# Two heads' 64-row matmuls issued as a pair, from the upper and lower half of TensorE's rows

## The chip, the core and the metric

The kernel runs on one core of a Trainium2 chip. The metric is the device time of one execution in microseconds (us); lower is better. A core has five engines that run their own instruction streams and meet at semaphores: TensorE (PE, with its weight loads shown apart as PEld), VectorE (DVE), ScalarE (ACT), GpSimd (POOL) and SyncE (SP, which issues DMAs).

## What is computed

Two transformer-like blocks of two layers each, for 512 tokens of width 1024, all in fp32. Two places matter here. Both contract over a head dimension of 64, so their matmuls use 64 of the 128 rows of the array.

```
# block 0 (attention of the first block) and block 1 (dsa_attention), 8 heads of 64 each
s = einsum('bqhd,bkhd->bqhk', q, k) * 64 ** -0.5      # masked, softmax, times v
# block 1 only: the index score which picks the keys of block 1's attention
logits = einsum('bqhd,bsd->bqhs', iq, ik) * 64 ** -0.5
score  = einsum('bqh,bqhs->bqs', iw, relu(logits))    # summed over 8 index heads, then top-k of keys
```

## The kernel before

Each engine's program is written out by hand and its order is fixed. A *unit* is one 1024x128 slice of a weight matrix: TensorE multiplies it with the activations in eight k-steps of three matmuls each (high and low parts of an fp32 value kept as two fp32r tensors, `hH` and `hL`), 128x512 each, line L1758. Units alternate between two PSUM banks (`ACC`), and a unit can start only when `acc_free` says that VectorE or ScalarE has read the bank two units back.

**Block 0 attention.** 32 *steps* per layer: step n is head `n % 2` of the head pair `n // 2 % 4` of the query tile `i = n // 8`. The keys of tile i are the first 128(i+1), so a score matmul is 128 queries by 128, 256, 384 or 512 keys. Three steps go into each unit from the 13th on, behind its k-steps 0, 3 and 6. In one call `attention(w, n)` TensorE issues the scores of step n (L1961, into `SC[n % 2]`, banks 3 and 4), the transposes of the probabilities of step n-1 (L1972), and the product with v of step n-2 (L1983). VectorE reads the scores (L1352), ScalarE takes the exponential (L939) and copies the transposed tile (L948). The head pair's two heads lie in partitions 0 to 63 and 64 to 127 of `qT` and `kT`.

**Block 1 attention.** The same 32 steps, after the last projection unit, with matmuls of the output projection put between (`half_step`, L1932 to L1934) and in the first 16 steps one dummy matmul (`keep_warm`, L1898) per step. VectorE also finishes the top-k search here (`top_round`, L1632 and L1635).

**Block 1 index logits.** 32 logits matmuls per layer, y = 8 i + head, each 128 queries by 128(i+1) keys (`index_logits`, L1864). They are put between the k-steps of units 6 to 10 and 12 by the table `IX_AT`: for a unit with m of them, behind the k-steps 7-m to 6. Logits y go to bank `PT` (5) or `OA` (6) by the parity of y, so TensorE waits at y for ScalarE's relu of y-2 (L1166). VectorE adds each into the score (L1616, L1618); it holds the relus back through four buffers `ir`. In VectorE's program the scores of unit u+1 stand ahead of its reading of unit u (`pool_window`, first instruction L1320), which in turn frees the bank that unit u+2 waits for. ScalarE's relus of a unit stand behind the copy (L885) of the result of the `pool_window` before. Unit 11 is replaced by `pool_mix`, which writes banks 2 and 7 (`MIX`).

Of the kernel before, what the change touches and what calls it, by code (L numbers as in the profile page):

```python
# [27 lines left out]
ACT = mybir.ActivationFunctionType  # L28
AX_X = mybir.AxisListType.X

P = 128
# [11 lines left out]
HD = 64  # L43
# [103 lines left out]


IX_AT, _y = {}, 0
for _u, _n in ((6, 3), (7, 6), (8, 6), (9, 6), (10, 6), (12, 5)):  # L150
    IX_AT[_u] = tuple(range(_y, _y + _n))
    _y += _n
assert _y == 32


TOP_AT, TOP_STEPS, _r, _r3 = {}, {}, 0, 0
for _u in range(10, IN2):
    _n, _n3 = 1 + (_u >= 18), int(_u >= 12)
# [115 lines left out]
def build(nc, d):  # L274
    ctx = ExitStack()
    with ctx:
# [65 lines left out]
        with ExitStack() as share:  # L342
# [4 lines left out]
            iqT = sb("iqT", [P, 4, S], F32, share)  # L347
            ikT = sb("ikT", [P, S], F32, share)
            bias2 = sb("bias2", [P, 10 * P], F32, share)
            ir = sb("ir", [P, 4, S], F32, share)  # L350
# [19 lines left out]
        STAT = bank[2]  # L370
        DB = bank[0:3]
        SC = bank[3:5]
        PT, OA, TRO = bank[5:8]
        OSUM, R1, WARM = bank[5], bank[6], bank[4]
        THIRD, FOURTH = bank[5], bank[7]
        MIX = (bank[2], bank[7])

        def cst(name, a=0, b=None):
            o, n = CAT[name]
# [42 lines left out]
        turn_done = signal("turn_done", 12, 17, 2)  # L422
        sc_done = signal("sc_done", 32, 32)
        sc_read = signal("sc_read", 32, 32, 2)
# [32 lines left out]
        ix_done = signal("ix_done", 0, 32)  # L457
        ix_relu = signal("ix_relu", 0, 32)
# [53 lines left out]
        def att_step(n):  # L512

            return n // 2 % 4, n // 8, n % 2
# [327 lines left out]
        def _(act):  # L842
# [170 lines left out]
            for L in range(LAYERS):  # L1013
                w = Where(0, L)
                norm(w, 0)
                fourth_high(w, 0)
                for u in range(24):
# [27 lines left out]
                    if u in (19, 23):  # L1045
                        i = (u - 19) // 4
# [99 lines left out]
                for k in range(KD):  # L1146
                    for u in range(2):
                        y = 3 * k + u
                        next_high(w, 40 + y // 2, y % 2)
                    y = 3 * k + 2  # L1150
# [6 lines left out]
            for L in range(LAYERS):  # L1157
                w = Where(1, L)
                norm(w, 0)
                fourth_high(w, 0)  # L1160
                for u in range(IN2):
                    for y in IX_AT.get(u, ()):
                        wd = P * (y // 8 + 1)
                        act.wait_ge(ix_done.sem, ix_done.at(w, y + 1))
                        act.wait_ge(ix_used.sem, ix_used.at(w, y - 3))
                        act.activation(ir[:, y % 4, 0:wd], (PT, OA)[y % 2][:, 0:wd], ACT.Relu,  # L1166
                                       scale=HD ** -0.5).then_inc(ix_relu.sem, 1)
                    j = turn_of(1, u)
                    if j is not None:
                        turn_input(w, j, u // 2, u % 2, acc_of(w, u)[0], HD ** -0.5 if 5 <= j < 9 else 1.0)  # L1170
                    if u >= 2:
                        high_of(w, u + 2)
                    if 0 < u - POOL_U <= 4:
                        g = u - POOL_U - 1
                        piece_high(w, N_PD2 + g, piece[:, g % 2, :], pdH[:, g, :])
                    if u in (WPOOL + 1, WPOOL + 2):
                        for g in (0, 1) if u == WPOOL + 1 else (2, 3):
                            piece_high(w, N_PY2 + g, piece[:, g % 2, :], pdH[:, g, :])
                for n in range(SLOTS):
                    for h in HALVES_AT[n - 1] if n else ():  # L1180
                        first_half(w, h)
                    attention(w, n)
                use_table(ROOT)
                second_halves(w)
                output_root(w, 0)
                next_high(w, 14, 1)
                norm(w, 1)

                def hidden(c, i, s):

                    bk, n = (33 + s) % 2, N_HID2 + HCH * c + s
                    act.wait_ge(acc_free[bk].sem, acc_free[bk].at(w, i + 12 * c + 18 + s + 1))
                    act.wait_ge(piece_lo.sem, piece_lo.at(w, i * 2 + n - 1))
                    act.activation(piece[:, s, :], relu[:, s, :], ACT.Square).then_inc(piece_ready.sem, 1)  # L1194
                    act.activation(hidH2[:, bass.ds(i * 2 + s, 1), :], relu[:, s, :],
                                   ACT.Square).then_inc(piece_hi.sem, 1)

                fourth_high(w, 1)
                hidden(0, 0, 0)
                hidden(0, 0, 1)  # L1200
                for c in range(FCHUNKS):
                    with act.Fori(1 - c, HCH // 2) as i:
                        for s in range(2):
                            hidden(c, i, s)
                            next_high(w, i + 15 + 16 * c, s)
                    for k in range(KD):
                        bk = (49 + k) % 2
                        next_high(w, k + 23 + 16 * c, 0)
                        unit_wait(w, k + 23 + 16 * c, 1)
                        if c == 0:  # L1210
                            act.activation(mT2[:, k, :], ACC[bk][:, :], ACT.Copy).then_inc(acc_free[bk].sem, 1)
                        else:

                            act.wait_ge(acc_free[bk].sem, acc_free[bk].at(w, k // 2 + 12 * c + 26 + k % 2 + 1))
                            square(w, SQ_OUT[1][1] + k, k % 2, mT2[:, k, :])
                        if c == 0 or k < KD - 1:
                            next_high(w, k + 23 + 16 * c, 1)
                output_root(w, 1)
                next_high(w, 46, 1)
# [3 lines left out]
        def _(dve):  # L1223
# [297 lines left out]
            for L in range(LAYERS):  # L1521
                w = Where(0, L)
# [159 lines left out]
            for L in range(LAYERS):  # L1682
                w = Where(1, L)
                dve.wait_ge(rope_ready, 1)
                norm_scales(w)
                for u in range(IN2):
                    if u == 0:
                        copy_gates(w)
                    if u == 2:
                        gate_scale(w)  # L1690
                    for y in IX_AT.get(u + 1, ()):
                        index_score(w, y)
                    j = turn_of(1, u)
                    if j is not None:
                        turn_finish(w, j)
                    elif u != WPOOL:
                        pool_window(w, u - POOL_U)
                    if u in (WPOOL, WPOOL + 1):
                        for g in (0, 1) if u == WPOOL else (2, 3):
                            pool_scaled(w, g)  # L1700
                    for rounds in TOP_AT.get(u, ()):
                        top_round(rounds)
# [35 lines left out]
        def _(pe):  # L1738
# [115 lines left out]
                pe.wait_ge(sq_ready.sem, sq_ready.at(w, 8 + c + 1))  # L1854
                pe.matmul(STAT[:, :], cst("ones"), sq[:, c % 2, :], start=True, stop=True).then_inc(sq_used.sem, 1)

            def index_logits(w, y):
                i, h = y // 8, y % 8
                if y == 0:
                    pe.wait_ge(turn_done.sem, turn_done.at(w, 5))  # L1860
                if y >= 2:
                    pe.wait_ge(ix_relu.sem, ix_relu.at(w, y - 1))
                p0 = h % 2 * HD
                pe.matmul((PT, OA)[y % 2][:, 0:P * (i + 1)], iqT[p0:p0 + HD, h // 2, i * P:i * P + P],  # L1864
                          ikT[p0:p0 + HD, 0:P * (i + 1)], start=True, stop=True).then_inc(ix_done.sem, 1)

            def turn(w, j):
                src = turn_src(w.b, j)
# [31 lines left out]
            def pool_mix(w, g):  # L1900

                if g == 0:
                    pe.wait_ge(w_lo.sem, w_lo.at(w, WPOOL + 1))
                pe.wait_ge(piece_lo.sem, piece_lo.at(w, N_PD2 + g + 1))
                if g >= 2:
                    pe.wait_ge(piece_ready.sem, piece_ready.at(w, N_PY2 + g - 1))
                c = g * P
                pe.matmul(MIX[g % 2][:, :], pwH[:, c:c + P], pdH[:, g, :], start=True, stop=False)
                pe.matmul(MIX[g % 2][:, :], pwL[:, c:c + P], pdH[:, g, :], start=False, stop=False)
                pe.matmul(MIX[g % 2][:, :], pwH[:, c:c + P], pdL[:, g, :], start=False,  # L1910
                          stop=True).then_inc(unit_done.sem if g == 1 else pool_done.sem, 1)
# [40 lines left out]
            def attention(w, n, fill=()):  # L1952
                q, k, v, sc, pt, ao, st, _, n0 = ATT[w.b]

                for n_ in (n,) if n < 32 else ():
                    f, i, h = att_step(n_)
                    if n_ == 0:
                        pe.wait_ge(turn_done.sem, turn_done.at(w, (12, 17)[w.b]))
                    if 1:
                        pe.wait_ge(sc_read.sem, sc_read.at(w, n - 1))  # L1960
                    pe.matmul(SC[n_ % 2][:, 0:P * (i + 1)], q[h * HD:h * HD + HD, f, i * P:i * P + P],  # L1961
                              k[h * HD:h * HD + HD, f, 0:P * (i + 1)], start=True, stop=True).then_inc(sc_done.sem, 1)
                for i in fill[0:1]:
                    half_step(w, i // 4, i % 4, 0)
                m = n - 1
                if 0 <= m < 32:
                    f, i, h = att_step(m)
# [9 lines left out]
                if 0 <= m < 32:  # L1977
                    f, i, h = att_step(m)
# [115 lines left out]
            with pe.Fori(0, LAYERS) as L:  # L2094
                w = Where(0, L)
# [57 lines left out]
                with pe.Fori(0, KD // 2) as i:  # L2153
                    for m in range(2):
                        for u in range(3):
                            y = 3 * m + u
# [126 lines left out]
```

## Time and profile before

| | us |
|---|---|
| median of 3 runs | 3181.61 (3181.59 to 3187.2) |
| the profiled execution | 3177.61 |
| its span in the trace | 3175.6 |
| PE busy | 3011.6 (95% of the span) |
| DVE, ACT, POOL busy | 1252.0, 1147.7, 1246.4 |
| mean granted TensorE clock | 0.96 of full |

The profiled execution is 4.0 us below the median of the runs. Busy time of an engine is the time in which it has an instruction in work; waits stand apart. A granted clock of 1.00 is 2.4 GHz, 0.50 is 1.2 GHz.

### The profile page before, as it was taken

How to read it: one execution, taken by the hardware profiler on the slowest of the kernel's cores; microseconds unless marked ns; L12 is line 12 of the kernel's file. 1: busy time of each engine (PE TensorE's matmuls, PEld its weight loads, DVE VectorE, ACT ScalarE, POOL GpSimd, SP SyncE). 2: the span in 40 equal slices, each digit the busy share in tenths (PEclk: the TensorE clock that was granted, in tenths of full speed). 3: DMA queues.
4: the chain of work that ended last, by engine and by line, in shares of the span. 5: the costliest groups of instructions: out<-in, count | busy, mean ns of one | idle time of the engine just before them, and what ended most of it. 6: DMA issues, size and time to landing. Idle time of an engine off the chain costs nothing.

```text
span 3175.6 us, 42194 instructions
## 1 busy us (share of the span) xinstructions
PE 3011.6 (95%) x14156; PEld 2368.0 (75%) x14156; DVE 1252.0 (39%) x2240; ACT 1147.7 (36%) x1894; POOL 1246.4 (39%) x626
## 2 busy tenths in 40 slices
PE   9998899999999989999999998999999999999997
PEld 7767877788877678778888656678878656688876
DVE  4455426553064444265521467330012557330012
ACT  4453134443234522344433223542233223542331
POOL 3313123555432131235554343145553343145553
PEclk9999899999999988999999989999999989999999
DMA  3211012223311100112333111122222111022222
GB/s 128 67 41 34 1 40 67 93 94 100 104 64 66 40 27 1 47 67 93 99 99 100 56 47 54 34 73 93 92 93 86 58 44 60 31 72 97 92 93 93
DMA packets 62869, 217.35 MB, mean 68 GB/s; under 512 B 6577, under 2 KB 6705, under 8 KB 62481
## 3 DMA queue, kind: packets, MB, share of 16 engines
q1 hardware_dynamic: 62416, 214.48, 20.4%
q8 instruction: 82, 1.34, 0.2%
q0 software_dynamic: 320, 1.12, 0.1%
q14 instruction: 51, 0.41, 0.0%
HBM read 213.48 MB, written 2.10 MB: 68 GB/s over the span
## 4 chain that ended last, share of the span: by engine, by line
PE 80%; DVE 7%; POOL 4%; ACT 4%; issue 3%; DVEq 1%; ACTq 0%; DMA 0%; POOLq 0%; SPq 0%
PE bank L1758 48%; PE bank L2059 5%; POOL wL L681 3%; PE bank L1961 3%; PE bank L1932 2%; PE bank L1807 2%; PE bank L1785 2%; PE bank L1983 2%; PE bank L1933 2%; PE bank L1934 2%; PE bank L1864 1%; PE bank L1972 1%; ACT wH L850 1%; PE bank L1815 1%; PE bank L1872 1%
## 5 line engine op out<-in xcount | busy, mean ns | idle before, releaser
L681 POOL TENSOR_TENSOR wL<-raw,wH 128x1024 fp32r<-128x1024 f32 x380 | 920.2, 2422 | 1409.0 <-ACT wH L850 1409.0
L1758 PE MATMUL bank<-hH,wH 128*128 128x512 f32 x1744 | 728.9, 418 | 23.4 <-POOL wL L681 17.6
L1758 PE MATMUL bank<-hL,wH 128*128 128x512 f32 x1744 | 687.2, 394 | 0.0
L1758 PE MATMUL bank<-hH,wL 128*128 128x512 f32 x1744 | 686.9, 394 | 0.0
L850 ACT ACTIVATE wH<-raw 128x1024 fp32r<-128x1024 f32 x380 | 399.4, 1051 | 278.6 <-PE bank L1758 238.3
L1758 PEld LDWEIGHTS bank<-hH,wH 128*128 128x128 f32 x1744 | 331.5, 190 | 164.1 <-issue 87.4
L1758 PEld LDWEIGHTS bank<-hL,wH 128*128 128x128 f32 x1744 | 331.5, 190 | 72.2
L1758 PEld LDWEIGHTS bank<-hH,wL 128*128 128x128 f32 x1744 | 332.4, 191 | 69.2 <-issue 10.5
L1758 PE MATMUL bank<-hidH,wH 128*128 128x512 f32 x864 | 338.1, 391 | 2.4 <-POOL wL L681 2.3
L1758 PE MATMUL bank<-hidH,wL 128*128 128x512 f32 x864 | 336.3, 389 | 0.0
L1758 PE MATMUL bank<-hidL,wH 128*128 128x512 f32 x864 | 336.3, 389 | 0.0
L1717 DVE SCALAR_TENSOR_TENSOR relu<-bank,rstd 128x512 f32<-128x512 f32 x64 | 44.1, 692 | 479.8 <-PE bank L1758 467.8
L1758 PEld LDWEIGHTS bank<-hidH,wH 128*128 128x128 f32 x864 | 162.1, 188 | 41.9 <-issue 7.5
L1758 PEld LDWEIGHTS bank<-hidL,wH 128*128 128x128 f32 x864 | 162.2, 188 | 34.0
L1758 PEld LDWEIGHTS bank<-hidH,wL 128*128 128x128 f32 x864 | 162.2, 188 | 33.0
L1588 DVE SCALAR_TENSOR_TENSOR mT<-bank,par,mT 128x511 f32<-128x511 f32 (+1 forms) x176 | 131.9, 749 | 111.0 <-ACT mT L1127 96.5
L714 POOL TENSOR_TENSOR hidL<-piece,hidH 128x512 f32 (+1 forms) x108 | 139.5, 1293 | 75.7 <-ACT hidH L885 75.2
L939 ACT ACTIVATE sc<-sc,st 128x128 f32<-128x128 f32 (+3 forms) x128 | 71.9, 562 | 185.2 <-DVEq L1355 184.7
L1194 ACT ACTIVATE piece<-relu 128x512 f32<-128x512 f32 x64 | 40.4, 632 | 216.3 <-DVE relu L1717 215.6
L1961 PE MATMUL bank<-kT,qT 64*128 64x128 f32 (+3 forms) x256 | 104.1, 487 | 14.1 <-DVE v L1339 14.1
L726 POOL TENSOR_TENSOR eb<-ab,const 128x512 f32<-128x512 f32 x40 | 50.1, 1268 | 147.3 <-PE bank L2059 84.3
L1127 ACT ACTIVATE mT<-bank,par 128x512 f32<-128x512 f32 x88 | 68.5, 779 | 98.5 <-DVE bank L1584 94.2
(323 smaller groups left out, 4287.1 us busy)
## 6 DMA issues: line engine op xcount, KB each, us to landing
raw<-w_dram SPq DMA_DIRECT2D x398, 512.0 KB, 3.4
x<-x_dram SPq DMA_DIRECT2D x4, 512.0 KB, 9.0
out_dram<-x SPq DMA_DIRECT2D x1, 2048.0 KB, 6.2
const<-const_dram SPq DMA_DIRECT2D x1, 1421.0 KB, 12.8
par_next<-par_dram POOLq DMA_DIRECT2D x5, 168.0 KB, 2.6
qkT<-pos_dram POOLq DMA_DIRECT2D x1, 256.0 KB, 7.0
const<-const_dram SPq DMA_DIRECT2D x1, 131.0 KB, 2.2
```

The costliest lines, as they stand in the source:

```text
L681: pool.tensor_tensor(wL[:, s, :], raw[:, s, :], wH[:, s, :].bitcast(F32), ALU.subtract).then_inc(w_lo.sem, 1)
L714: pool.tensor_tensor(dst, shape(src), hi.bitcast(F32), ALU.subtract).then_inc(piece_lo.sem, 1)
L850: act.activation(wH[:, s, :], raw[:, s, :], ACT.Copy).then_inc(w_hi.sem, 1)
L939: act.activation(sc[:, n % 2, 0:wd], sc[:, n % 2, 0:wd], ACT.Exp, bias=st[:, MN + n % 4:MN + n % 4 + 1], scale=-1.0, accum_out=st[:, SUM + ...
L1127: act.activation(mT1[:, 2 * q + s, :], banks[s][:, :], ACT.Identity, bias=prmd(w, "fbias", i * 4 + 2 * q + s), scale=prmd(w, "fconv", i * ...
L1588: last = dve.scalar_tensor_tensor(buf[:, lag:S], banks[s][:, 0:S - lag], prmd(w, "fconv", i * 12 + 6 * q + 3 * s + 2 - lag), buf[:, lag:S] ...
L1758: mm = pe.matmul((out or ACC[bk])[:, :], wt[:, s, c:c + P], rhs, start=first and k == 0 and j == 0, stop=last and k == tiles - 1 and j == 2)
L1785: mm = pe.matmul(bank_[:, t:t + 1], squares[:, t * P:t * P + P], cst("ones", 0, 1), start=first and t == 0, stop=last and t == NT - 1)
L1807: pe.matmul(ACC[banks[s]][:, :], wt[:, s, c:c + P], hH[:, k, :], start=k == 0 and j == 0, stop=False)
L1932: pe.matmul(out[:, :], wH[:, p % 2, c:c + P], high, start=k == 0, stop=False)
L1961: pe.matmul(SC[n_ % 2][:, 0:P * (i + 1)], q[h * HD:h * HD + HD, f, i * P:i * P + P], k[h * HD:h * HD + HD, f, 0:P * (i + 1)], start=True, ...
L2059: mm = pe.matmul(o, two[h][0], two[h][1], start=True, stop=True)
```

## The change

Scores and index logits of the two heads of a pair are issued one right behind the other. The first head's operands lie in partitions 0 to 63 and the second's in 64 to 127, and they write to different banks. In attention the two score matmuls stand at the even step, under one wait for all earlier scores to be read; the odd step issues none. The index logits go in 16 pairs of y's; pairs use banks 5 and 6, and 2 and 7, in turn (the last two pairs banks 5 and 6 only), so a pair waits for the relus of the pair two back. The table now puts 2 or 3 pairs into a unit in place of up to 6 single ones, and `pool_mix` waits for 28 relus, since its banks are now shared.

```
-for _u, _n in ((6, 3), (7, 6), (8, 6), (9, 6), (10, 6), (12, 5)):
+for _u, _n in ((6, 2), (7, 3), (8, 3), (9, 3), (10, 3), (12, 2)):
...
+        def index_bank(y):
+            pair = y // 2
+            return ((PT, OA), (STAT, TRO))[pair % 2 if pair < 14 else 0][y % 2]
...
-            def index_logits(w, y):
-                i, h = y // 8, y % 8
...
-                if y >= 2:
-                    pe.wait_ge(ix_relu.sem, ix_relu.at(w, y - 1))
...
+            def index_logits(w, pair):
...
+                if pair >= 2:
+                    pe.wait_ge(ix_relu.sem, ix_relu.at(w, 2 * pair - 2 * (pair < 15)))
+                i = pair // 4
+                for y in (2 * pair, 2 * pair + 1):
+                    p0, f = y % 2 * HD, y % 8 // 2
+                    pe.matmul(index_bank(y)[:, 0:P * (i + 1)], iqT[p0:p0 + HD, f, i * P:i * P + P],
+                              ikT[p0:p0 + HD, 0:P * (i + 1)], start=True, stop=True).then_inc(ix_done.sem, 1)
...
                 if g == 0:
                     pe.wait_ge(w_lo.sem, w_lo.at(w, WPOOL + 1))
+                    pe.wait_ge(ix_relu.sem, ix_relu.at(w, 28))
...
-                    if 1:
-                        pe.wait_ge(sc_read.sem, sc_read.at(w, n - 1))
-                    pe.matmul(SC[n_ % 2][:, 0:P * (i + 1)], q[h * HD:h * HD + HD, f, i * P:i * P + P],
-                              k[h * HD:h * HD + HD, f, 0:P * (i + 1)], start=True, stop=True).then_inc(sc_done.sem, 1)
...
+                if n < 32 and n % 2 == 0:
+                    pe.wait_ge(sc_read.sem, sc_read.at(w, n))
+                    f, i, _ = att_step(n)
+                    for h in range(2):
+                        pe.matmul(SC[h][:, 0:P * (i + 1)], q[h * HD:h * HD + HD, f, i * P:i * P + P],
+                                  k[h * HD:h * HD + HD, f, 0:P * (i + 1)], start=True,
+                                  stop=True).then_inc(sc_done.sem, 1)
```

TensorE's instructions in a unit of block 0 that carries attention steps of tile i = 1, before (`bank3` and `bank4` are the two score banks, `bank5` the transposes, `bank6` the product with v):

```order
L1960 REGISTER_ALU
L1961 MATMUL bank4<-kT1,qT1 128x256
L1972 MATMUL bank5<-const,sc1 128x128 x2
L1983 MATMUL bank6<-v1,pt1 128x64
L1758 MATMUL bank0<-hH,wH 128x512
```

The same place now (the changed file's lines; L1970 is L1961 before, L1982 is L1972, L1993 is L1983 and L1764 is L1758):

```order
L1967 REGISTER_ALU
L1970 MATMUL bank3<-kT1,qT1 128x256
L1970 MATMUL bank4<-kT1,qT1 128x256
L1982 MATMUL bank5<-const,sc1 128x128 x2
L1993 MATMUL bank6<-v1,pt1 128x64 x2
L2001 MATMUL bank7<-const,eb1 128x128
L1764 MATMUL bank0<-hH,wH 128x512
```

One step of the pair now has both score matmuls, and the other goes from the unit's matmuls straight to the transposes.

TensorE's instructions in unit 7 of block 1, where index logits stand between the k-steps, before (`bank1` is the unit's own bank):

```order
L1758 MATMUL bank1<-hL,wH 128x512
L1862 REGISTER_ALU
L1864 MATMUL bank6<-ikT,iqT 128x128
L1758 MATMUL bank1<-hH,wH 128x512
L1758 MATMUL bank1<-hH,wL 128x512
L1758 MATMUL bank1<-hL,wH 128x512
L1862 REGISTER_ALU
L1864 MATMUL bank5<-ikT,iqT 128x128
```

And now, in the same unit (L1872 is L1864 before):

```order
L1872 MATMUL bank5<-ikT,iqT 128x128
L1872 MATMUL bank6<-ikT,iqT 128x128
L1764 MATMUL bank1<-hH,wH 128x512
L1764 MATMUL bank1<-hH,wL 128x512
L1764 MATMUL bank1<-hL,wH 128x512
L1868 REGISTER_ALU
L1872 MATMUL bank2<-ikT,iqT 128x128
L1872 MATMUL bank7<-ikT,iqT 128x128
```

The unit holds three such pairs, behind its k-steps 4, 5 and 6, where six single matmuls stood behind the k-steps 1 to 6.

## Rows read from the trace of the kernel before

**Rows 1.** The page: TensorE's busy time, and the chain that ended last by engine.

```profile
PE 3011.6 (95%) x14156; PEld 2368.0 (75%) x14156; DVE 1252.0 (39%) x2240; ACT 1147.7 (36%) x1894; POOL 1246.4 (39%) x626
...
PE 80%; DVE 7%; POOL 4%; ACT 4%; issue 3%; DVEq 1%; ACTq 0%; DMA 0%; POOLq 0%; SPq 0%
```

**Rows 2.** Busy time by stretch; the last three columns are clock, DMA share, GB/s.

```profile
103.00:238.00 135.00, 129.83 (x611) 88.63 (x609) 69.03 (x199) 71.87 (x172) 28.68 (x12) 0.99 0.14 48
972.00:1105.00 133.00, 127.87 (x597) 87.66 (x598) 68.74 (x199) 72.51 (x174) 26.30 (x11) 0.97 0.14 44
1797.00:1890.00 93.00, 84.42 (x237) 44.31 (x237) 53.49 (x92) 26.02 (x50) 28.68 (x16) 0.85 0.14 46
1947.00:2058.00 111.00, 103.60 (x507) 75.50 (x508) 46.83 (x179) 55.72 (x151) 17.08 (x9) 0.92 0.07 24
2507.00:2600.00 93.00, 82.82 (x224) 42.54 (x225) 54.01 (x91) 25.31 (x48) 28.05 (x16) 0.83 0.14 46
1819.10:1833.00 13.90, 13.70 (x28) 7.17 (x27) 7.49 (x11) 2.59 (x5) 3.15 (x2) 0.51 0.00 0
1855.20:1868.60 13.40, 13.40 (x25) 6.61 (x25) 4.71 (x5) 4.13 (x6) 2.88 (x2) 0.57 0.01 1
```

**Rows 3.** The two groups of 64-row matmuls, by line, with their shapes.

```profile
L1961 PE MATMUL bank<-kT,qT x256: 271/482/693, 109.4 to 2742.2; 64*128 64x128 f32 x32, 64*128 64x256 f32 x32, 64*128 64x384 f32 x32, 64*128 64x512 f32 x32
L1864 PE MATMUL bank<-ikT,iqT x128: 272/483/1220, 1797.2 to 2590.4; 64*128 64x128 f32 x32, 64*128 64x256 f32 x32, 64*128 64x384 f32 x32, 64*128 64x512 f32 x32
```

**Rows 4.** The chain that ended last, in the index stage: start, us, what.

```profile
1798.53 0.41 PE bank L1864 x2
...
1809.63 0.89 PE bank L1758 x3
1810.53 0.62 PE bank L1864 x2
...
1839.43 0.84 PE bank L1864 x2
...
1870.61 1.05 PE bank L1864 x2
```

**Rows 5.** The same chain in block 0's attention stage.

```profile
214.03 0.70 PE bank L1758 x3
...
232.61 1.05 PE bank L1961 x2
233.66 0.59 PE bank L1972 x4
...
237.20 0.44 PE bank L1972 x4
```

**Rows 6.** Weight loads by time: start, us, then idle before.

```profile
1836.74 0.19 PEld L1758 LDWEIGHTS bank<-hH,wH 128*128 128x128 f32 x1 [0.55 <-issue]
1836.84 0.19 PEld L1758 LDWEIGHTS bank<-hH,wL 128*128 128x128 f32 x1
```

**Rows 7.** The chain at eight 64-row records of one row half, 128 columns each.

```profile
420.85 1.08 PE bank L2082 x8
```

**Rows 8.** TensorE's waits: index stage of both layers, then the attention stage's start (us, times, longest).

```profile
PE bank L1864 <- ACT ir L1166: 4.0, 4, 2.4
...
PE bank L1864 <- ACT ir L1166: 5.3, 4, 1.9
...
PE bank L1961 <- DVE v L1339: 7.5, 1, 7.5
```

**Rows 9.** The end of a unit with index logits, all engines by time.

```profile
1842.04 0.49 ACT L1166 ACTIVATE ir<-bank 128x384 f32<-128x384 f32 x1 [1.24 <-PE bank L1864]
1842.57 0.62 DVE L1618 SCALAR_TENSOR_TENSOR bias<-ir,iw,bias 128x384 f32<-128x384 f32 x1 [1.11 <-ACT ir L1166]
1843.28 0.69 DVE L1320 TENSOR_TENSOR pu<-bank,rstd 128x512 f32<-128x512 f32 x1
1844.02 0.50 PE L1758 MATMUL bank<-hH,wH 128*128 128x512 f32 x1 [1.12 <-DVE pu L1320]
```

More of the change, by code:

```diff
@@ L149 @@
 IX_AT, _y = {}, 0
-for _u, _n in ((6, 3), (7, 6), (8, 6), (9, 6), (10, 6), (12, 5)):
+for _u, _n in ((6, 2), (7, 3), (8, 3), (9, 3), (10, 3), (12, 2)):
     IX_AT[_u] = tuple(range(_y, _y + _n))
     _y += _n
-assert _y == 32
+assert _y == 16
 TOP_AT, TOP_STEPS, _r, _r3 = {}, {}, 0, 0
@@ L1161, in _ @@
                 for u in range(IN2):
-                    for y in IX_AT.get(u, ()):
+                    for y in (2 * pair + h for pair in IX_AT.get(u, ()) for h in range(2)):
                         wd = P * (y // 8 + 1)
@@ L1165, in _ @@
                         act.wait_ge(ix_used.sem, ix_used.at(w, y - 3))
-                        act.activation(ir[:, y % 4, 0:wd], (PT, OA)[y % 2][:, 0:wd], ACT.Relu,
+                        act.activation(ir[:, y % 4, 0:wd], index_bank(y)[:, 0:wd], ACT.Relu,
                                        scale=HD ** -0.5).then_inc(ix_relu.sem, 1)
@@ L1690, in _ @@
                         gate_scale(w)
-                    for y in IX_AT.get(u + 1, ()):
+                    for y in (2 * pair + h for pair in IX_AT.get(u + 1, ()) for h in range(2)):
                         index_score(w, y)
@@ L1855, in l2_sum @@
                 pe.matmul(STAT[:, :], cst("ones"), sq[:, c % 2, :], start=True, stop=True).then_inc(sq_used.sem, 1)
-            def index_logits(w, y):
-                i, h = y // 8, y % 8
-                if y == 0:
+            def index_logits(w, pair):
+                if pair == 0:
                     pe.wait_ge(turn_done.sem, turn_done.at(w, 5))
-                if y >= 2:
-                    pe.wait_ge(ix_relu.sem, ix_relu.at(w, y - 1))
-                p0 = h % 2 * HD
-                pe.matmul((PT, OA)[y % 2][:, 0:P * (i + 1)], iqT[p0:p0 + HD, h // 2, i * P:i * P + P],
-                          ikT[p0:p0 + HD, 0:P * (i + 1)], start=True, stop=True).then_inc(ix_done.sem, 1)
+                if pair >= 2:
[5 more added lines that the diff above has]
+                              ikT[p0:p0 + HD, 0:P * (i + 1)], start=True, stop=True).then_inc(ix_done.sem, 1)
             def turn(w, j):
@@ L1953, in attention @@
                 q, k, v, sc, pt, ao, st, _, n0 = ATT[w.b]
[L1955 to L1958, printed above, removed]
-                    if 1:
-                        pe.wait_ge(sc_read.sem, sc_read.at(w, n - 1))
-                    pe.matmul(SC[n_ % 2][:, 0:P * (i + 1)], q[h * HD:h * HD + HD, f, i * P:i * P + P],
-                              k[h * HD:h * HD + HD, f, 0:P * (i + 1)], start=True, stop=True).then_inc(sc_done.sem, 1)
+                if n == 0:
+                    pe.wait_ge(turn_done.sem, turn_done.at(w, (12, 17)[w.b]))
+                if n < 32 and n % 2 == 0:
[5 more added lines that the diff above has]
+                                  stop=True).then_inc(sc_done.sem, 1)
                 for i in fill[0:1]:
```

## The prediction

> **What bounds the kernel now.** I read the page first, to see whether TensorE is what the end waits for: it is busy 95% of the span and makes up 80% of the chain that ended last [rows 1]. A kernel can be bound by TensorE as a whole and yet not in the stages that a change touches, so the second view is busy time by stretch. The change touches three stages, each run once per layer. In block 0's attention stage TensorE is busy 129.8 of 135 us in one layer and 127.9 of 133 in the other; VectorE and ScalarE are near half busy. In block 1's attention stage it is 103.6 of 111. In the index stage it is 84.4 of 93 and 82.8 of 93, while VectorE has 53.5 and 54.0 [rows 2]. The reader should see that TensorE sets the time in all three, the index stage least clearly. The third view is the waits. In the index stages TensorE stood 4.0 and 5.3 us behind ScalarE's relus, and once 7.5 us behind VectorE ahead of block 1's first score [rows 8]. The same stretches show the clock: 0.99 and 0.97 in block 0's attention, but 0.85 and 0.83 in the index stages. Two pieces of the first layer's index stage, 13.9 and 13.4 us long, ran at 0.51 and 0.57, so nearly all at 1.2 GHz [rows 2].
>
> **What a single 64-row matmul costs.** There are 384 records of them, two for each matmul: 128 score matmuls and 64 index matmuls [rows 3], so 64 and 32 pairs, in equal parts with 128, 256, 384 and 512 columns. On the chain one takes 0.41, 0.62, 0.84 and 1.05 us for these four widths [rows 4]. That is 0.213 us per 128 columns, half of it in each record, plus a fixed 0.20. The three unit matmuls behind one take 0.89 us, and three without one before them 0.70 [rows 4, 5]: another 0.19. So an index matmul costs 0.39 us beside its columns. In block 0's attention the transposes behind a score matmul take 0.59 us and those of the first step that has none 0.44 [rows 5]; its fixed part is 0.20 + 0.15 = 0.35. The fixed part is a wait for the array to empty and for weights that were not loaded ahead, on entering and leaving the 64-row form.
>
> **Term 1, one entry and exit for two heads.** The second head of a pair follows a matmul of its own form. Eight such records of 128 columns, in one row half, take 1.08 us [rows 7], 0.135 each against 0.107 of columns, so the second head's two records keep some 0.05 of cost where they are narrow, and I take 0.04 over all widths. Saved: 0.31 on each of 64 score pairs = 19.8 us, and 0.35 on each of 32 index pairs = 11.2.
>
> **Term 2, the two halves at once.** No row shows two row halves side by side. The records go in order: first head first and second record, then the second head's. If only different halves may overlap, the second record of head one runs beside the first record of head two; one record of four is hidden. Its length is 0.107, 0.213, 0.32 or 0.427 us. It cannot start at once, for weight loads follow each other by 0.10 us [rows 6]. That leaves 0, 0.11, 0.22, 0.33, mean 0.165, times 96 = 15.8 us. The bounds: nothing (the halves run one after the other), and both records of the second head hidden, mean 0.53, times 96 = 51 us. I take the middle because the queue is in order and the two records of one head need the same half; nothing in these rows excludes either end. The Trainium skill, page "TensorE: Matmul & The Clock Gate", section on the measured speedup of packed matmuls, gives a pack the length of one matmul plus some 4 ns per further tile. By that a pair of two-record matmuls in this order would hide one record of four without my 0.10 delay, an estimate of 0.27 a pair and 25.6 us in all; and if the pack counts a whole fp32 matmul, it is my upper bound.
>
> **Term 3, waits of the index stage.** With four banks a pair waits for relus two pairs back. The 4.0 and 5.3 us behind the relus [rows 8] should go, since these waits come when ScalarE is held up behind a `pool_window`, now covered by the first five k-steps, which carry no logits. Against it: at a unit's end relu, score and the bank read follow each other, 0.49, 0.62 and 0.69 us, while TensorE waits 1.12 [rows 9]. With a pair behind k-step 6 a second relu and score stand in that chain; the first head's overlap with the second's matmul, so some 0.5 us more at each of four unit ends in two layers: 4 us. `pool_mix`, now behind 28 relus, and the last pair, behind the relus of the one before, wait about 0.7 us each: 3 us for both layers. Net gain 9.3 - 7 = 2 us. Queued behind those waits is only TensorE's own next unit. VectorE's work is unchanged, 53 us in 93.
>
> **Term 4, the clock.** In the slow pieces TensorE is nearly always busy [rows 2]. About 8 us of the first is timed by TensorE (the rest by VectorE's `pool_window`) and all of the second, so they cost some 4 and 6.7 us, 10.7 a layer. Ahead of both falls TensorE had waited for relus. Those waits go but others come at the unit ends. I take half of it as returned, 11 us in two layers; bounds 0 and 21.
>
> **Term 5, what is taken back.** The sc_read wait at the even step now asks for the score before it too, but that score is issued a whole step earlier than before, so its read is earlier as well: cost nothing, covered by the step between. If VectorE were late there (top-k rounds of block 1), both scores would be late together, at most a read of 0.7 us a pair. In the first twelve steps of block 1's attention VectorE's rounds leave little slack, and the 7.5 us wait before them is VectorE's [rows 8]. I take back 4 us for both layers.
>
> **Sum.** 19.8 + 11.2 + 15.8 + 2 + 11 - 4 = 55.8 us. From the profiled execution's 3177.6 this is 3121.8; the median of the runs lies 4.0 higher, so I predict 3125.8.
>
> **Rivals.** (a) *The halves don't overlap*: term 2 is nil, 3142; with no clock returned 3153. For it: no row shows an overlap. Chance 0.22. (b) *Both records overlap*: 35 us more, 3091. Against it: the two records of one head share a half and the queue is in order. Chance 0.08. (c) *VectorE and ScalarE become the bound of the index stage*: each unit then takes `pool_window`, copy, relus and six scores in a row, and terms 1, 3 and 4 of that stage and its third of term 2 are lost, 11 + 2 + 11 + 5 = 29 us: 3155. For it: scores now bunch behind k-step 4. Against it: VectorE is idle for 40 of 93 us. Chance 0.10. The skill's page "TensorEngine Tiling (Array Packing)", section PSUM Bottleneck, warns of this: tiling speeds up the matmuls, not the reading of PSUM. (d) *Nothing*: the second head still empties the array, since the fixed part belongs to a change of half as much as to one of form. Then terms 1 and 2 are nil and the bunched logits save and cost about the same: 3175 to 3185. Chance 0.05. (e) *Slower, by the clock*: pairs keep half the array idle for up to 2 us in a row. If the attention stages fall as the index stage does, where 27 of 93 us ran slow, then of their 490 us (twice 134 and twice 111) 142 run at half clock and lose 71 us: 3125.8 + 71 = 3197. It decides from 112 us of added slow time. Against it: block 0's attention holds 0.99 with as many 64-row matmuls. Chance 0.06.
>
> **How the numbers follow.** The forecast has 0.49. Its own range, with the bounds of term 4 and of the delay in term 2, is 3105 to 3140. The cases (a) and (c) lie up to 3155, (b) at 3091; 3093 to 3157 leaves out (b) in part, (d) and (e), less than 2 in 10. A measurement of this kernel tells about 0.2%, 6.4 us, from no change. Faster: all but (d), (e) and the worst of (c), 0.88; same 0.05; slower 0.07.
>
> **What would show it.** Score pairs on the chain: about 0.6 us for 128 columns and 1.6 for 512, if one record is hidden (0.20 + 3 x 0.427 + 0.10); 1.9 for 512 if none; 1.05 if two. Transposes at odd steps at 0.44. No wait for L1166's relus ahead of logits, but one of 1.5 to 2 us on `pu` at the ends of units 7 to 10. A clock of 0.90 or more in the index stages. The prediction is wrong if a pair takes twice a single, if stretches at 1.2 GHz appear in block 0's attention, or if the index stage stays at 93 us with VectorE busy throughout.

## The result and the profile after

The changed kernel takes 3090.3 us (median of 4 runs, 3085.2 to 3100.8) where the kernel before takes 3181.6 on the same chip: a ratio of 0.9714 with a 95% interval of 0.9684 to 0.9743, 91 us less. The forecast was 3125.8, so 35 us of gain were not foreseen; the time lies 2.7 us below the range, where rival (b) put it. The profiled execution went from 3177.6 to 3093.4, 84.2 us less and 28.4 below the 3121.8 that the forecast had for it. The readings below are of these two.

The page of the changed kernel has the same order of engines [rows 1]:

```profile
PE 2918.5 (94%) x14156; PEld 2346.1 (76%) x14156; DVE 1229.9 (40%) x2240; ACT 1143.7 (37%) x1894; POOL 1247.3 (40%) x626
...
PE 80%; DVE 6%; ACT 4%; POOL 4%; issue 3%; DVEq 1%; ACTq 0%; DMA 0%; POOLq 0%; SPq 0%
```

TensorE has 93 us less busy time in as many instructions, and no other engine took its place. To see where, I cut both traces into stages at landmarks: from the first score or first index logits of a layer to the first instruction of the next stage. The rows give length, then busy time and count of PE, PEld, DVE, ACT and POOL, then granted clock, DMA share and GB/s. Before: block 0's first attention, and block 1's index stage (up to the first score) and attention, of both layers:

```profile
109.40:239.10 129.70, 124.85 (x588) 84.90 (x589) 67.55 (x196) 71.16 (x171) 26.29 (x11) 0.99 0.14 45
1797.20:1947.90 150.70, 134.40 (x455) 83.69 (x454) 107.67 (x209) 40.38 (x68) 61.22 (x32) 0.89 0.18 60
1947.90:2074.50 126.60, 117.62 (x589) 87.40 (x589) 55.24 (x190) 62.27 (x161) 24.27 (x12) 0.93 0.09 30
2506.90:2659.50 152.60, 136.23 (x454) 84.33 (x453) 100.57 (x209) 40.48 (x68) 61.53 (x32) 0.89 0.18 59
2659.50:2784.90 125.40, 118.23 (x589) 88.38 (x589) 55.42 (x190) 62.38 (x161) 24.25 (x12) 0.92 0.10 31
```

The same five stages of the changed kernel:

```profile
109.70:226.80 117.10, 111.02 (x588) 81.90 (x589) 66.75 (x196) 70.67 (x172) 26.36 (x11) 0.99 0.16 50
...
1774.20:1904.20 130.00, 111.29 (x451) 77.69 (x450) 96.77 (x209) 39.07 (x68) 61.63 (x32) 0.95 0.21 69
1904.20:2021.60 117.40, 107.50 (x589) 84.97 (x589) 52.98 (x190) 62.49 (x161) 24.35 (x12) 0.90 0.10 33
2453.40:2583.60 130.20, 111.47 (x452) 77.76 (x451) 97.16 (x209) 39.08 (x68) 61.64 (x32) 0.95 0.21 69
2583.60:2700.90 117.30, 107.36 (x588) 84.92 (x589) 52.81 (x190) 62.42 (x161) 24.37 (x12) 0.90 0.10 33
```

Block 0's attention gained 12.6 us in this layer and 13.7 in the other (130.7 to 117.0), the index stages 20.7 and 22.4, block 1's attention 9.2 and 8.1. That is 86.7; the other stages gave back the remaining 2.5. Per layer the prediction's terms had put 7.6 into block 0's attention, 14.7 into the index stage and 5.6 into block 1's attention, so all three gained more than forecast (5 to 6, 6 to 8, 2.5 to 3.6 us).

The direct test is the pair itself. The chain that ended last, at pairs of 512 columns in block 0 and of 384 and 512 in the index stage (start, us, what; answers to [rows 4, 5]):

```profile
206.01 0.44 PE bank L1982 x4
...
209.41 1.06 PE bank L1970 x4
210.47 0.58 PE bank L1982 x4
```

```profile
1817.32 0.84 PE bank L1872 x4
1818.16 0.89 PE bank L1764 x3
1819.06 1.06 PE bank L1872 x4
```

Four records take 1.06 us where two took 1.05 before. I had expected 1.6. The second head of a pair costs 0.01 us at any width that I read: 0.42, 0.63, 0.85 and 1.06 for a pair, 0.41, 0.62, 0.84 and 1.05 for a single. What follows costs what it did, 0.89 for three unit matmuls and 0.58 for the transposes, and steps without scores have their transposes at 0.44. The timeline shows how. TensorE in the 0.03 us after 209.33, and in the whole stretch around:

```profile
209.34 0.70 PE L1970 MATMUL bank<-kT,qT 64*128 64x512 f32 x2
```

```profile
209.34 1.13 PE L1970 MATMUL bank<-kT,qT 64*128 64x512 f32 x4
```

And in the stretch from 210.1 on, where the first two have ended:

```profile
209.88 0.60 PE L1970 MATMUL bank<-kT,qT 64*128 64x512 f32 x2
```

Two of the four records start together at 209.34; the other two start at 209.88, 0.54 later. Only the last record of a matmul raises the semaphore `sc_done`, and in the trace both raises stand on the two records at 209.88. So each couple is one record of either head. With both heads in one row half (below), the raises stand on the second and the fourth record; if that is the order of the program here too, the first record of head two passes the second of head one. The weight loads go the same way: the first ones of the two heads start within 0.01 us of each other, the second ones 0.11 later.

### The profile page after: what moved, and what is told of

Same layout as the page of the kernel before. It is cut to its first block, busy times and chain, and to the rows that moved or that the text cites. A ratio compares the mean times of both kernels' runs of the same rounds, so it can differ in the third digit from the quotient of the medians.

```text
span 3091.6 us, 42164 instructions
## 1 busy us (share of the span) xinstructions
PE 2918.5 (94%) x14156; PEld 2346.1 (76%) x14156; DVE 1229.9 (40%) x2240; ACT 1143.7 (37%) x1894; POOL 1247.3 (40%) x626
## 3 DMA queue, kind: packets, MB, share of 16 engines
q1 hardware_dynamic: 62416, 214.48, 20.7%
## 4 chain that ended last, share of the span: by engine, by line
PE 80%; DVE 6%; ACT 4%; POOL 4%; issue 3%; DVEq 1%; ACTq 0%; DMA 0%; POOLq 0%; SPq 0%
PE bank L1764 50%; PE bank L2069 5%; POOL wL L687 3%; PE bank L1941 2%; PE bank L1813 2%; PE bank L1791 2%; PE bank L1942 2%; PE bank L1943 2%; PE bank L1993 2%; ACT wH L856 1%; PE bank L1982 1%; PE bank L1970 1%; PE bank L1880 1%; PE bank L1821 1%; PE bank L1906 1%
## 5 line engine op out<-in xcount | busy, mean ns | idle before, releaser
L1764 PE MATMUL bank<-hH,wH 128*128 128x512 f32 x1744 | 723.8, 415 | 36.6 <-POOL wL L687 19.1
L1764 PE MATMUL bank<-hH,wL 128*128 128x512 f32 x1744 | 686.6, 394 | 0.0
L1764 PE MATMUL bank<-hL,wH 128*128 128x512 f32 x1744 | 686.2, 393 | 0.0
L1764 PEld LDWEIGHTS bank<-hH,wH 128*128 128x128 f32 x1744 | 331.6, 190 | 158.1 <-issue 66.6
L1764 PEld LDWEIGHTS bank<-hH,wL 128*128 128x128 f32 x1744 | 332.0, 190 | 71.2 <-issue 10.5
L1764 PEld LDWEIGHTS bank<-hL,wH 128*128 128x128 f32 x1744 | 331.2, 190 | 71.9
L1764 PE MATMUL bank<-hidH,wH 128*128 128x512 f32 x864 | 338.2, 391 | 2.4 <-POOL wL L687 2.3
L1764 PE MATMUL bank<-hidH,wL 128*128 128x512 f32 x864 | 336.4, 389 | 0.0
L1764 PE MATMUL bank<-hidL,wH 128*128 128x512 f32 x864 | 336.4, 389 | 0.0
L1764 PEld LDWEIGHTS bank<-hidH,wH 128*128 128x128 f32 x864 | 162.2, 188 | 42.1 <-issue 7.5
L1764 PEld LDWEIGHTS bank<-hidL,wH 128*128 128x128 f32 x864 | 162.2, 188 | 34.0
L1764 PEld LDWEIGHTS bank<-hidH,wL 128*128 128x128 f32 x864 | 162.2, 188 | 32.7
L1590 DVE TENSOR_TENSOR bank<-bank,rstd 128x512 f32<-128x512 f32 x88 | 61.5, 699 | 96.9 <-PE bank L1764 86.1
```

Of the source, the lines that this page charges most:

```text
L1764: mm = pe.matmul((out or ACC[bk])[:, :], wt[:, s, c:c + P], rhs, start=first and k == 0 and j == 0, stop=last and k == tiles - 1 and j == 2)
```

## The experiments

The first four kernels ran beside each other on one chip; their kernel before took 3186.9 us (3170.9 to 3199.1, 7 runs).

**Attention alone.** The kernel before with paired scores; index logits and their banks as before.

```
-                for n_ in (n,) if n < 32 else ():
...
+                if n < 32 and n % 2 == 0:
+                    pe.wait_ge(sc_read.sem, sc_read.at(w, n))
+                    f, i, _ = att_step(n)
+                    for h in range(2):
+                        pe.matmul(SC[h][:, 0:P * (i + 1)], ...
```

> The kernel before with only the attention scores paired, in both blocks. Theory O (the two row halves run fully side by side, so a pair costs what a single costs): the four attention stages gain together 12.6 + 13.7 + 9.2 + 8.0 = about 43 us as in the trace of the changed kernel, so 3138 us. Rival C (a good part of the whole gain is the index stage's clock and waits, and the attention stages gained only because they came after a changed index stage): block 1's attention keeps its 126 us, gain about 26 us, 3155.

3144.5 us (3126.7 to 3148.7), ratio 0.9845 [0.9792, 0.9898]. Block 1's attention took 115.9 and 117.1 us, so its gain does not need a changed index stage ahead of it.

**Index alone.** The changed kernel with the single scores of before in attention (the same lines, the other way round).

> The changed kernel with the attention scores as before: only the index logits are paired, with four banks. Theory O: 32 pairs save 0.39 + 0.53 us each, 29 us, and the waits and the clock of the index stage give 10 to 15 more: 3138 us, each index stage some 20 us shorter. Rival: if the index gain is mostly pairs, 3152; if mostly clock, the stage's length changes between its two layers by several us.

3152.3 us (3148.5 to 3153.5), ratio 0.9884 [0.9839, 0.9929]. The ratios stand for 49 and 37 us, 86 together, against 91 for both at once: the two halves of the change add up within the intervals. In the traces attention alone shortens block 0's attention stage to 117.0, and index alone shortens the index stages to 130.1 and 127.6 and leaves block 0's attention at 130.6. Index alone gives some of its gain back behind them, in block 1's attention, whose instructions are those of before:

```profile
1941.10:2071.60 130.50, 122.44 (x589) 91.58 (x589) 55.37 (x190) 62.90 (x161) 24.26 (x12) 0.89 0.09 30
```

It takes 130.5 us where it took 126.6, with 28 us at 1.2 GHz in place of 18; the other layer shows the same, 130.4 for 125.4.

**Both heads in the same row half.** What this kernel leaves out is said in its expectation.

```
-                    p0, f = y % 2 * HD, y % 8 // 2
+                    p0, f = 0, y % 8 // 2
...
-                        pe.matmul(SC[h][:, 0:P * (i + 1)], q[h * HD:h * HD + HD, f, i * P:i * P + P],
-                                  k[h * HD:h * HD + HD, f, 0:P * (i + 1)], start=True,
+                        pe.matmul(SC[h][:, 0:P * (i + 1)], q[0:HD, f, i * P:i * P + P],
+                                  k[0:HD, f, 0:P * (i + 1)], start=True,
```

> The changed kernel, but both matmuls of a pair take their operands from partitions 0 to 63: the second head's scores and logits are computed from the first head's q and k, so the output is not the reference's. Order, banks and waits are those of the changed kernel. Theory O: the overlap is gone, each pair grows by the columns of one matmul, mean 0.53 us, 96 pairs: 51 us, so 3141 us, and a pair of 512 columns takes 1.9 us on the chain where it took 1.06. Rival A (being adjacent, not the two halves, made the second head cheap): 3090 us and 1.06. Rival R (one record of four was hidden, the rest came from elsewhere): 16 us more, 3106.

3125.4 us (3112.8 to 3130.9), ratio 0.9798 [0.9747, 0.985]. The chain, a pair of 512 columns in block 0:

```profile
226.19 1.91 PE bank L1970 x4
228.10 0.59 PE bank L1982 x4
```

In this stretch no record starts with another: they start 0.43 to 0.53 us apart. Block 0's attention and block 1's index stage, of the first layer:

```profile
122.40:245.30 122.90, 118.59 (x588) 87.09 (x589) 66.88 (x196) 71.70 (x171) 26.30 (x11) 0.99 0.15 48
1787.90:1921.70 133.80, 119.83 (x452) 83.04 (x451) 98.45 (x209) 40.46 (x68) 62.45 (x32) 0.95 0.20 67
```

1.91 is 0.20 + 4 x 0.427: one entry, four records in a row. So term 1 holds with only the halves made equal, the halves make the whole difference of 0.85 us to 1.06, and that is both records of the second head. But the stages show less than TensorE does. Against this kernel the changed one has TensorE busy 8.5 us less in the index stage (119.8 to 111.3, 16 pairs at 0.53), and the stage is 3.8 shorter: TensorE stood 8.6 us behind `pu` (L1326) where it stood 4.4 here. In the other layer, where this kernel's clock was the higher (0.98 against 0.95), the changed kernel's stage is even 1.5 longer. In block 0's attention 7.6 of busy time became 5.8. Over all stages that the edit touches the overlap gave 28 us, and the ratios differ by 0.0084, 27 us, of the 51 us that 96 pairs at 0.53 take out of TensorE's work.

**Two banks again.** The changed kernel with pairs in banks 5 and 6 only; `pool_mix` no longer waits for relus.

```
-            return ((PT, OA), (STAT, TRO))[pair % 2 if pair < 14 else 0][y % 2]
+            return (PT, OA)[y % 2]
...
-                if pair >= 2:
-                    pe.wait_ge(ix_relu.sem, ix_relu.at(w, 2 * pair - 2 * (pair < 15)))
+                if pair >= 1:
+                    pe.wait_ge(ix_relu.sem, ix_relu.at(w, 2 * pair))
```

> The changed kernel with the index pairs in banks 5 and 6 only, so that a pair waits for both relus of the pair before, and without the wait of pool_mix. Theory W (the banks gave about what my term 3 said): each of 32 pairs waits 0.1 to 0.4 us, 3093 to 3103 us. Rival: the banks are most of the index stage's extra gain, since the first pair of a unit waits for a ScalarE that is held up behind the pool window: 10 us a layer, 3110 us.

3104.8 us (3092.8 to 3114.3), ratio 0.9726 [0.9678, 0.9774], which holds the changed kernel's 0.9714. Its index stages took 130.3 and 130.7 us, against 130.0 and 130.2. TensorE's waits in the first (engine, line, released by: us, times, longest):

```profile
PE bank L1764 <- DVE pu L1326: 6.5, 4, 1.9
...
PE bank L1872 <- ACT ir L1172: 2.2, 4, 1.4
```

and in the changed kernel:

```profile
PE bank L1764 <- DVE pu L1326: 8.6, 4, 3.9
...
PE bank L1872 <- ACT ir L1172: 0.3, 1, 0.3
```

The sum is 8.7 and 8.9. With pairs, two more banks change where TensorE waits and not how long. So pairs late in the unit, in two banks, have all but 0.5 us of the index stages' gain.

That left open why the index stage gained 7 us more than forecast, the clock's part in it, and whether the place of the logits or the banks took the relu waits away. The next four ran together (kernel before 3177.1 us, 3167.0 to 3187.3, 8 runs).

**Four banks with single logits.** The kernel before, logits at their old places, in four banks; `pool_mix` waits for 27 relus.

```
+        def ix_bank(y):
+            return (PT, OA, STAT, TRO)[y % 4] if y < 27 else (PT, OA)[y % 2]
...
-                if y >= 2:
-                    pe.wait_ge(ix_relu.sem, ix_relu.at(w, y - 1))
+                if y >= 4:
+                    pe.wait_ge(ix_relu.sem, ix_relu.at(w, y - 3 if y < 27 else y - 1))
```

> The kernel before with its single index logits in four banks (5, 6, 2, 7 in turn up to y = 26, then 5 and 6), so that TensorE waits for the relu of y-4, not y-2; pool_mix waits for 27 relus. Theory B (the two more banks removed the waits behind ScalarE's relus): the 4.0 and 5.3 us go, index stages 5 us shorter each, 3172 us. Theory T (the place of the logits late in the unit removed them, not the banks): a single logit behind k-step 1 to 6 soon runs four ahead of a ScalarE that stands behind the pool window, so the stages stay within 2 us of 150.7 and 152.7.

3143.0 us (3140.0 to 3152.4), ratio 0.9896 [0.9864, 0.9929], 33 us. Its first index stage:

```profile
1809.60:1944.70 135.10, 122.23 (x454) 78.17 (x453) 98.36 (x209) 39.97 (x68) 62.10 (x32) 0.99 0.20 67
```

and TensorE's waits for VectorE and ScalarE in it; there is none for a relu:

```profile
PE bank L1762 <- DVE pu L1324: 3.4, 4, 1.1
PE bank L1913 <- DVE piece L1662: 1.8, 1, 1.8
...
PE bank L1880 <- ACT turn_in L935: 0.3, 1, 0.3
```

This was the surprise of the study: the banks alone, without any pair, shorten the stage by 15.6 us (17.5 in the other layer). The records are as many as before, and yet TensorE's busy time fell by 12.2 us, from 134.4 to 122.2, while its idle time fell by 3.4. With the work unchanged I put the fall of the busy time down to the clock, 0.89 before and 0.99 here. Time at 1.2 GHz is twice the missing share of the clock times the length: 33 us before, 3 to 4 here. In the kernel before, the two longest waits on relus of this stage stand just ahead of the two slow stretches from 1819.1 and from 1855.2 us on [rows 2]:

```profile
1818.49 0.71 PE L1864 MATMUL bank<-ikT,iqT 64*128 64x256 f32 x2 [0.99 <-ACT ir L1166]
...
1851.51 0.91 PE L1864 MATMUL bank<-ikT,iqT 64*128 64x384 f32 x2 [2.36 <-ACT ir L1166]
```

The run with attention alone, whose index stage is that of before, has two such slow stretches behind the same waits in its first layer; with four banks both waits and both stretches are gone, in both layers. So the slow stretches hang on the waits for relus [rows 8]. With single logits the banks matter; with pairs, by the run before, they do not. Either change takes these waits away. What placing the logits late does by itself has no run.

**The halves apart.** The changed kernel with the second head's logits behind the first unit matmul of the next k-step, so that nothing is paired; banks and waits stay.

```
+                        for n, small in enumerate(second):
+                            if j == 0 and k == n + tiles - len(second):
+                                small()
```

> The changed kernel, but the second logits matmul of each index pair stands behind the first unit matmul of the next k-step: same table, banks and waits, no sharing of entry and exit and no overlap. Attention as in the changed kernel. Theory P (what the index stage gained is pairs: 0.39 + 0.53 us on each of 16 a layer): index stages 15 us longer than the changed kernel's 130, 3119 us. Rival L (the placing late in the unit and the clock are most of the 20 us): 5 to 8 us longer a stage, 3103.

3109.0 us (3097.7 to 3116.1), ratio 0.9791 [0.9744, 0.9839]. Its index stages took 138.3 us each:

```profile
1769.60:1907.90 138.30, 124.39 (x452) 81.14 (x451) 100.55 (x209) 40.60 (x68) 61.93 (x32) 0.97 0.20 65
```

Pairing takes 16 x (0.39 + 0.53) = 14.7 us of TensorE's work out of this stage, and 8.3 and 8.1 us of time. With four banks, single logits at these late places are 3.2 us slower than at their old ones.

**VectorE's window first.** The changed kernel, but VectorE does `pool_window` of unit u ahead of the scores of unit u + 1, so the bank that TensorE waits for at a unit's end is read first.

```
+                    j = turn_of(1, u)
+                    if j is None and u != WPOOL:
+                        pool_window(w, u - POOL_U)
                     for y in (2 * pair + h for pair in IX_AT.get(u + 1, ()) for h in range(2)):
                         index_score(w, y)
...
-                    elif u != WPOOL:
-                        pool_window(w, u - POOL_U)
```

> The changed kernel with VectorE's order in block 1 changed: pool_window of unit u stands ahead of the index scores of unit u+1, so the unit's bank is read at once. Theory V (the waits on pu at the ends of units 7 to 10, 17.1 us in 8, are TensorE's loss): they go and 10 to 17 us are saved, 3073 to 3080. Rival: VectorE's chain of window and six scores per unit is the bound of the index stage, and the wait only moves to the relus: 3087 to 3093.

3085.5 us (3067.7 to 3088.0), ratio 0.9696 [0.9649, 0.9743].

**The same, with the pairs spread.** Behind the k-steps 1, 3 and 5 in place of 4, 5 and 6.

```
+                        unit(w, u // 2, ..., between=[...], at={6: (4, 5), 12: (2, 4)}.get(u, (1, 3, 5)))
```

> As window_first, with the three pairs of a unit behind k-steps 1, 3 and 5 in place of 4, 5 and 6 (4 and 5 in unit 6, 2 and 4 in unit 12). Theory V: same as window_first or some us less, since scores spread. Rival (ScalarE still stands behind the pool window when the third pair wants its bank): waits for relus come back, 5 us above window_first.

3086.4 us (3066.8 to 3089.1), ratio 0.97 [0.965, 0.975]. Both shorten the index stages, to 123.3 and 121.6 and to 123.8 and 123.7; the spread adds nothing. The medians could not tell them from the changed kernel, so the third set repeated that beside the better one (kernel before 3183.0 us, 3169.3 to 3189.8, 11 runs).

**The changed kernel again.**

> The changed kernel once more, beside window_first on one chip, since single executions here differ by some 12 us with a stretch at 1.2 GHz that starts in stages that no edit touches. 3085 to 3100 us; ratio to the kernel before 0.971.

3087.5 us (3084.3 to 3092.0, 5 runs), ratio 0.971 [0.9683, 0.9738].

**Window first again.**

> window_first once more beside it. Theory V: index stages 7 and 8.5 us shorter than in the changed kernel, 13 us in all less what the clock takes back: 3075 to 3085, below the changed kernel by 5 to 15. Rival: what it gains at the unit ends is returned later in the layer: no difference.

3079.9 us (3070.6 to 3088.4, 6 runs), ratio 0.9687 [0.9658, 0.9715]. The index stages of both layers, and what TensorE still waited for in the first:

```profile
1768.70:1890.10 121.40, 108.78 (x451) 75.89 (x450) 98.39 (x209) 38.90 (x68) 62.96 (x32) 0.97 0.23 74
2438.40:2561.00 122.60, 108.65 (x451) 76.33 (x450) 98.54 (x209) 38.90 (x68) 62.90 (x32) 0.96 0.22 73
```

```profile
...
PE bank L1917 <- ACT ir L1172: 1.8, 1, 1.8
PE bank L1872 <- ACT ir L1172: 1.4, 3, 0.9
```

The wait of 8.6 us on `pu` is gone; 3.2 us on relus stand in its place, and the stages are 8.6 and 7.6 us shorter. The medians differ by 7.5 us, half of the 16 that the stages promise, with intervals that overlap: a gain of the index stages in every profiled execution of that order, not settled by the times.

**Window first without the dummy matmuls.** The line `keep_warm(STAT, 1)` of the first 16 steps of block 1's attention is left out as well.

> window_first without the one dummy matmul in each of the first 16 attention steps of block 1 (it leaves out no part of the result). If the dummies only cost, 16 x 0.37 = 6 us a layer less: 3068 us. Rival, by the clock: the attention stage of block 1 idles more and runs longer at 1.2 GHz, and the gain is gone or turned: 3080 to 3095.

3084.0 us (3070.9 to 3101.4), ratio 0.9714 [0.9677, 0.9751]. The attention stages of both layers:

```profile
1896.20:2009.50 113.30, 102.41 (x557) 80.18 (x557) 53.52 (x190) 61.91 (x161) 24.40 (x12) 0.91 0.11 34
2562.70:2678.50 115.80, 105.42 (x557) 82.48 (x557) 53.58 (x190) 62.05 (x161) 24.38 (x12) 0.87 0.10 34
```

They have 32 records fewer and are 4.1 and 1.5 us shorter than the changed kernel's, 2.6 and 1.5 shorter than the 116.0 and 117.3 of window first again. The clock takes part of the gain back where it falls, to 0.87 and 30 us at 1.2 GHz in the second layer. No gain shows in the median.

**No top-k rounds.** The changed kernel without VectorE's rounds in block 1's attention; what that leaves out stands in the expectation.

```
-                    if n in TOP_STEPS:
-                        top_round(TOP_STEPS[n])
```

> The changed kernel without the six top-k rounds that stand among the attention steps of block 1 (the search of the last query tile stops after 10 of 16 rounds, so its mask is not the reference's). Theory D (VectorE's rounds took back the 5 us a layer by which block 1's attention gained less than block 0's): the stage is 4 to 6 us shorter in each layer than 117.3. Rival (the clock took it back: 24 us at 1.2 GHz against 18 before): within 2 us of 117.3, with the same slow stretches.

3097.1 us (3087.5 to 3105.3), ratio 0.9728 [0.9692, 0.9765]. The first layer's attention stage:

```profile
1918.20:2035.60 117.40, 107.48 (x589) 84.93 (x589) 44.27 (x170) 62.39 (x161) 24.11 (x12) 0.90 0.10 33
```

VectorE has 8.7 us less to do and the stage is as long to 0.1 us as the changed kernel's. The other layer's took 114.5 us with a clock of 0.94, where the changed kernel had 117.3. But the repeat of the changed kernel, with its rounds, shows the same two values:

```profile
1898.40:2015.80 117.40, 107.46 (x589) 84.95 (x589) 53.04 (x190) 62.55 (x161) 24.40 (x12) 0.90 0.10 33
2577.50:2691.90 114.40, 104.49 (x589) 82.63 (x589) 52.65 (x190) 62.40 (x161) 24.36 (x12) 0.94 0.10 34
```

So VectorE's rounds do not bound the stage, and the 3 us between the layers go with the clock.

## Why the prediction fell short

**What bounds the kernel** was read rightly: TensorE did, and less of its work made all three kinds of stage shorter.

**Term 1** (one entry and exit) holds. A pair in one row half costs 0.20 + 4 records, so the second head pays no entry; the 0.04 that I left on it is not there.

**Term 2 is the step that failed.** "I take the middle because the queue is in order and the two records of one head need the same half." The premise on the halves is right: 1.91 us where both heads share one. The conclusion from the queue is wrong: the second head's first record starts with the first head's first, so both its records are hidden, 51 us of TensorE's work and not 15.8. The delay of 0.10 us, read from loads of one form, did not hold between the halves either: there the loads start 0.01 us apart. Per stage term 2 was 5.9 us of TensorE's work short, against 5 to 8 us by which the stages of block 0's attention and of the index logits beat the forecast, and 2.5 to 3.6 in block 1's attention, where the clock took some back. The Trainium skill, page "TensorE: Matmul & The Clock Gate", section "Measured speedup vs the span model", gives a pack the length of one matmul plus about 4 ns for each further tile. The trace agrees if the pack counts whole fp32 matmuls: 1.06 us against 1.05. I had named that reading as my upper bound and set the in-order argument above it, with no row for either.

That the median missed by just these 35 us is partly chance. The profiled execution missed by 28.4, the overlap is worth some 28 us of time and not 51, and the other terms were off as well, in both directions:

**Term 4** was too small. I priced two slow stretches at 10.7 us a layer and returned half, 5.5. In the changed kernel the time at 1.2 GHz fell from 33 to 13 us. TensorE's busy time fell by 23.1 us in the first layer, 14.7 of them by pairs, so the clock returned some 8. With four banks and single logits it returned 12.2 and 14.0, more than I had priced in all. The waits on relus were a small loss themselves, 4 and 5 us, and stood ahead of a larger one.

**Term 3** was too kind. The waits on relus went, but TensorE's idle time in the first layer's stage still grew by 2.4 us, where I had 1 less. So 20.7 = 14.7 (pairs) + 8.4 (clock) - 2.4 (waits).

**The gains in the index stage do not add.** From the banks alone (135.1 us) to banks and pairs (130.0), 14.7 us of TensorE's work bought 5.1. TensorE's busy time fell by only 10.9, for the time at 1.2 GHz went from 4 to 13 us, and its idle time grew by 5.8, most of it in the waits on `pu`, 3.4 to 8.6. Term 3 had named this wait, at unit ends and on `pu`, with 2 us more a layer; it grew by 5.9, from this row of the kernel before to the 8.6 above:

```profile
PE bank L1758 <- DVE pu L1320: 2.7, 4, 1.1
```

Rival (c) as a bound of the whole stage did not come, since VectorE is busy 97 of 130 us, but its mechanism is what stops the rest of the gain. That VectorE's order is the cause of these waits is shown by the run that only puts its window first: they go, and 8 us come back.

**Term 5** took back 4 us for the wrong reason. In block 1's attention 9.2 and 8.1 of 14.1 us arrived, but not because of VectorE's rounds. In the first layer TensorE's busy time fell by 10.1 of the 14.1, since it ran 18 us at 1.2 GHz before and 24 now, and its idle time rose by 0.9; in the second these are 10.9 and 2.8. Two rows above show that the clock alone does this: index alone has a longer stage with the instructions of before, and the repeat of the changed kernel has 14 us at 1.2 GHz in one layer and a stage 3 us shorter. What makes the clock fall there is not shown. In block 0, where the clock stays at 0.99, 12.6 and 13.7 of 14.1 arrived.

**Rivals.** (a) falls with the two starts at 209.34, (d) with term 1, and (e) with the clock of block 0's attention. (b) happened. Its price of 35 us more than term 2 was right for TensorE's work; in time the overlap gave some 28 us in all, so that its 3091 lies beside the measured 3090.3 is partly luck.

## What to carry to other kernels

Two matmuls that contract over 64 rows can be issued back to back from the two row halves into two banks, and the second then cost TensorE 0.01 us here, also in fp32. So count it whole where TensorE sets the time, and look at once for what reads the results. A short wait in a stretch where TensorE is sparsely used should be priced with the clock that it may cost: here 4 us of waits stood before 12 us of slower matmuls. Price each part of a change by itself, but expect the sum of two parts that relieve one stage to be less: banks alone 16 us, pairs in two banks 20, both together 21.

## What was not expected of the hardware

TensorE runs the records of two fp32 matmuls side by side when their row halves differ: first with first at 209.34, second with second at 209.88. In one row half they ran one after the other, 0.43 us or more from start to start.

Executions of one kernel differ by some 12 us from a stretch at 1.2 GHz that comes in stages that no edit touches. The start of the program, before the first score, in the changed kernel and with attention alone:

```profile
0.00:109.70 109.70, 106.36 (x507) 84.75 (x507) 47.66 (x65) 43.61 (x61) 37.88 (x22) 0.98 0.33 116
```

```profile
0.00:122.90 122.90, 119.15 (x507) 95.90 (x507) 47.63 (x65) 43.56 (x61) 37.82 (x22) 0.88 0.30 104
```

The same 507 records take 13 us more at a clock of 0.88, some 30 us at 1.2 GHz. Eight of the twelve experiments' profiles show such a longer start (120 to 123 us), and the run with two banks shows another such stretch between block 1's layers. What starts it was not found. Single executions of one kernel differ by more than that here, so the stages of the trace, not the medians, carry the finer readings; and these too move by 1 to 3 us from one execution to the next with the clock.
